# Choosing the first head's experts beside the query projection, and turning the tokens to rows inside the expert stage

## What is computed

```python
qr = (h @ wq).reshape(bsz, t, PEER_HEADS, 2, PEER_HALF)          # 8 heads, 2 x 128 numbers each
scores = einsum('bthpd,hpkd->bthpk', qr, subkeys)                # 128 keys a half
s1, i1 = top_k(scores[..., 0, :], 16);  s2, i2 = top_k(scores[..., 1, :], 16)
cand = s1[..., :, None] + s2[..., None, :]                       # 256 candidates
top, pos = top_k(cand, 16);  eidx = (i1*128 + i2 at pos);  gate = softmax(top)
act = gelu(einsum('ted,td->te', u[eidx], h));  y = einsum('te,ted->td', gate * act, v[eidx])
```

## Time and profile before

| | us |
|---|---|
| median of 3 runs | 4855.84 (4854.93 to 4856.95) |
| the profiled execution, its own time | 4871.88 |
| its span, first to last instruction | 4870.1 |
| PE / DVE / ACT / POOL busy | 3931.9 / 3028.4 / 1902.0 / 1041.7 |
| layer 0: last query column copied to first gather | 693.91 to 716.15 |
| layer 0: gather stream, first issue to last product's start | 716.15 to 2012.90 |
| layer 1: last query column copied to first gather | 2380.08 to 2400.54 |
| layer 1: gather stream, first issue to last product's start | 2400.54 to 3050.28 |

### The profile page before, as it was taken

One profiled execution on the slowest core, in us unless ns is written; L12 is line 12 of the kernel. 1 busy time (PEld: TensorE's weight loads), 2 busy tenths in 40 slices (PEclk: granted clock), 3 DMA queues, 4 the chain that ended last, 5 costly groups with the idle time before them and its releaser, 6 DMA issues. The chain is left out here.

```text
span 4870.1 us, 55663 instructions
## 1 busy us (share of the span) xinstructions
PE 3931.9 (81%) x19683; PEld 2814.8 (58%) x19683; DVE 3028.4 (62%) x6110; ACT 1902.0 (39%) x4173; POOL 1041.7 (21%) x950
## 2 busy tenths in 40 slices
PE   7895677777777777785777777799989998899999
PEld 3574563223232232385532222679988987898899
DVE  7567546676666666467666665546566573565564
ACT  7532313333333333342333333444434353444543
POOL 0006104444344444104144443000010003000000
PEclk9996799999999999997899999979999997899999
DMA  9420139999999999531599999315534550254244
GB/s 374 151 87 0 44 110 421 421 420 417 415 413 418 415 413 418 229 113 32 189 421 421 417 418 415 108 48 165 157 104 135 161 161 5 70 166 148 77 156 139
DMA packets 205623, 1143.57 MB, mean 235 GB/s; under 512 B 23953, under 2 KB 25489, under 8 KB 106529
## 3 DMA queue, kind: packets, MB, share of 16 engines
q0 software_dynamic: 110592, 805.36, 40.0%
q1 hardware_dynamic: 94752, 334.65, 21.0%
HBM read 1138.87 MB, written 1.05 MB: 234 GB/s over the span
## 5 line engine op out<-in xcount | busy, mean ns | idle before, releaser
L1182 PE MATMUL bank<-rows,diag 128*128 128x512 f32 x2304 | 1080.8, 614 | 390.7 <-ACT diag L1237 383.9
L396 PE MATMUL bank<-x_high,w_high 128*128 128x272 f32 (+3 forms) x3560 | 1115.8, 313 | 96.7 <-DVE x_low L479 60.5
L396 PE MATMUL bank<-x_high,w_low 128*128 128x272 f32 (+3 forms) x3560 | 1096.8, 308 | 0.0
L396 PE MATMUL bank<-x_low,w_high 128*128 128x272 f32 (+3 forms) x3560 | 1094.4, 307 | 0.0
L1182 PEld LDWEIGHTS bank<-rows,diag 128*128 128x128 f32 x2304 | 422.7, 193 | 1041.8 <-ACT diag L1237 596.3
L1354 DVE CUSTOM_DVE_ANT_0 junk<-rows,hT 128x1024 f32<-128x1024 f32 x576 | 705.5, 1225 | 408.7 <-DMA rows<-in_peer_uv,expert 398.8
L421 ACT CAST w_high<-ring 128x1024 fp32r<-128x1024 f32 (+2 forms) x541 | 555.9, 1029 | 910.2 <-PE bank L396 897.3
L464 DVE TENSOR_TENSOR w_low<-ring,w_high 128x1024 fp32r<-128x1024 f32 (+2 forms) x541 | 647.8, 1199 | 373.6 <-ACT w_high L421 372.2
L1145 POOL DMA_INDIRECT rows<-in_peer_uv,expert x576 | 612.7, 1064 | 1139.4 <-PE bank L1182 797.2
L396 PEld LDWEIGHTS bank<-x_high,w_high 128*128 128x128 f32 (+1 forms) x3560 | 681.2, 191 | 149.5 <-issue 75.0
L396 PEld LDWEIGHTS bank<-x_low,w_high 128*128 128x128 f32 (+1 forms) x3560 | 682.5, 192 | 23.1
(11 more groups left out here) (394 smaller groups left out, 4601.6 us busy)
## 6 DMA issues: line engine op xcount, KB each, us to landing
ring<-in_w_gate_up SPq DMA_DIRECT2D x176, 512.0 KB, 3.3
ring<-in_w_mod SPq DMA_DIRECT2D x96, 512.0 KB, 5.4
ring<-in_w_in SPq DMA_DIRECT2D x64, 512.0 KB, 3.4
ring<-in_fox_w_in SPq DMA_DIRECT2D x64, 512.0 KB, 3.4
ring<-in_w_down SPq DMA_DIRECT2D x64, 512.0 KB, 3.5
ring<-in_peer_wq SPq DMA_DIRECT2D x32, 512.0 KB, 3.3
ring<-in_gdn_w_in SPq DMA_DIRECT2D x32, 512.0 KB, 3.8
ring<-in_w_down SPq DMA_DIRECT2D x32, 384.0 KB, 3.7
```

The costliest lines, as they stand in the source:

```text
L396: last = pe.matmul(k.bank[c % outs_banks][0:m, 0:nt], w[:, slot, cols], xx[:, t, t0:t0 + nt], start=(t == 0 and n_pass == 0), stop=(t == K ...
L1182: last = pe.matmul(k.bank[2 * (i % 2) + half][:, :], diag[:, n % 4, :], slot(n)[:, D + half * 512:D + (half + 1) * 512], start=(e == 0), s ...
```

## The change

- A class `Choice` holds the keys, the scores and the tiles of the choice; they are allocated before the two streams instead of within the expert stage. Its `choose` is the old one, with `yield 0` for `yield`.
- `stream` gets an SP side. In `peer_wq` SP loads the keys first; PE, after unit 5, forms the scores of head 0's two halves for tile 0; ACT copies them; DVE runs `choose(0)` in pieces.
- The stage `h_rows` is gone. In the expert stage PE turns the tokens to rows after the scores of tile 0, four 128 x 128 blocks to a bank, and ACT copies each bank (128 x 512) to `hT`: eight groups in layer 0, four in layer 1.
- POOL no longer waits for head 0. Gathers 6 and 7, which land in `k.H`, wait until `k.H` is turned (`hrows`). DVE's first product and PE's first sum wait for that too. ACT does head 0's exponentials before the copies of the scores.

```diff
 def stream(k, name, outs, x, evict, signals="", ..., pool_side=None, sp_side=None):
...
         @block.sync
         def _(sp):
+            if sp_side is not None:
+                sp_side(sp, s)
             for u in range(made_from, made_to):
                 sp.wait_ge(k.low_made, count(u))
...
         qr = sbuf(k, es, "qr", [P, 2 * PEER_HEADS, T])
+        choice = Choice(k, es)
...
+            def sp_side(sp, s):
+                sp.dma_start(choice.keys[:, :, :], a.peer_subkeys[l]).then_inc(s.keys, 16)
+
+            def pe_side(pe, s):
+                yield 2
+                pe.wait_ge(s.keys, 16)
+                pe.wait_ge(s.took, 2)
+                for c in range(2):
+                    last = pe.matmul(k.bank[SIDE_BANKS[0]][:, c * P:(c + 1) * P], qr[:, c, 0:P], choice.keys[:, c, :], start=True, stop=True)
+                last.then_inc(s.scored, 1)
+
+            def act_side(act, s):
+                yield 4
+                act.wait_ge(s.scored, 1)
+                act.copy(choice.scores[:, 0:2, :], k.bank[SIDE_BANKS[0]][:, 0:2 * P].rearrange("p (c n) -> p c n", c=2)).then_inc(s.scores, 1)
+
+            def dve_side(dve, s):
+                yield 5
+                dve.wait_ge(s.scores, 1)
+                choice.steps = 0
+                yield from choice.choose(dve, s, 0)
+
             stream(k, "peer_wq", ...,
+                   signals="keys scored scores step spread chosen", pe_side=pe_side, act_side=act_side, dve_side=dve_side, sp_side=sp_side)
-        transpose_chunks(k, "h_rows", [(hT[:, i, c * P:(c + 1) * P], H[:, c, t * P:(t + 1) * P])
-                                       for i, t in enumerate(tiles) for c in range(KD)])
...
-        @block.sync
-        def _(sp):
-            sp.dma_start(keys[:, :, :], a.peer_subkeys[l]).then_inc(s.keys, 16)
...
-                if e % TOPK == 0:
-                    pool.wait_ge(s.chosen, n // TOPK + 1)
+                if e % TOPK == 0 and n > 0:
+                    pool.wait_ge(s.chosen, n // TOPK)
+                if n == SLOTS - 2:
+                    pool.wait_ge(s.hrows, len(groups))
...
-            pe.wait_ge(s.keys, 16)
             score(0)
+            for j, (i, half) in enumerate(groups):
+                if j >= 4:
+                    pe.wait_ge(s.hrows, j - 3)
+                for c in range(4):
+                    last = pe.transpose(k.bank[j % 4][:, c * P:(c + 1) * P], k.H[:, 4 * half + c, tiles[i] * P:(tiles[i] + 1) * P], k.ident)
+                last.then_inc(s.hturned, 1)
...
+            exps(0)
             for n in range(4):
                 take_scores(0, n)
-            exps(0)
+            for j, (i, half) in enumerate(groups):
+                act.wait_ge(s.hturned, j + 1)
+                act.copy(hT[:, i, half * 512:(half + 1) * 512], k.bank[j % 4][:, :]).then_inc(s.hrows, 1)
...
-            for _ in choose(0):
-                pass
             for _ in choose(1):
                 pass
             weigh(0)
...
                 dve.wait_ge(landed[n % SLOTS], 16 * (n // SLOTS + 1))
+                if n == 0:
+                    dve.wait_ge(s.hrows, len(groups))
```

More of the change, by code:

```diff
@@ L1081, in peer, with peer_experts @@
             residual_project(k, "w_out", H, k.mods[:, l, 16:24, :], (1,) if l == DEPTH - 1 else (0, 1))
+            def sp_side(sp, s):
[4 more added lines that the diff above has]
+                pe.wait_ge(s.took, 2)
+                for c in range(2):
+                    last = pe.matmul(k.bank[SIDE_BANKS[0]][:, c * P:(c + 1) * P], qr[:, c, 0:P], choice.keys[:, c, :], start=True, stop=True)
[9 more added lines that the diff above has]
+                yield from choice.choose(dve, s, 0)
             stream(k, "peer_wq", [(1, P, 0, T)] * (2 * PEER_HEADS), H[:, :, T0:T0 + T],
-                   lambda dve, c, bank, s: dve.tensor_copy(qr[:, c, :], bank[:, 0:T]), norm=norm, ahead=False)
+                   lambda dve, c, bank, s: dve.tensor_copy(qr[:, c, :], bank[:, 0:T]), norm=norm, ahead=False,
+                   signals="keys scored scores step spread chosen", pe_side=pe_side, act_side=act_side, dve_side=dve_side, sp_side=sp_side)
         hT = sbuf(k, es, "hT", [P, len(tiles), D])
-        transpose_chunks(k, "h_rows", [(hT[:, i, c * P:(c + 1) * P], H[:, c, t * P:(t + 1) * P])
-                                       for i, t in enumerate(tiles) for c in range(KD)])
-        peer_experts(k, a, l, tiles, qr, hT)
-def peer_experts(k, a, l, tiles, qr, hT):
+        peer_experts(k, a, l, tiles, qr, hT, choice)
+def peer_experts(k, a, l, tiles, qr, hT, choice):
     NH = 2 * PEER_HEADS
@@ L1100, in peer_experts @@
     slots = " ".join(f"landed{n}" for n in range(SLOTS))
-    with ExitStack() as es, stage(k, "experts", slots + " keys scored took step chosen spread grown weights dotted "
+    with ExitStack() as es, stage(k, "experts", slots + " hturned hrows scored took step chosen spread grown weights dotted "
                                   "gelu weighed diag summed out_rows turned added") as (block, s):
         landed = [s.landed0, s.landed1, s.landed2, s.landed3, s.landed4, s.landed5, s.landed6, s.landed7]
-        keys = sbuf(k, es, "subkeys", [P, NH, N_KEYS])
-        scores = sbuf(k, es, "scores", [P, NH, N_KEYS])
         rows = sbuf(k, es, "rows", [P, SLOTS - 2, 2 * D])
@@ L1127, in peer_experts @@
         table = a.peer_uv[l]
+        keys, scores, expert, top, lowest = choice.keys, choice.scores, choice.expert, choice.top, choice.lowest
+        groups = [(i, n) for i in range(NT) for n in range(2)]
         def slot(n):
@@ L1180, in _ @@
                 pe.wait_ge(s.diag, n + 1)
+                if n == 0:
+                    pe.wait_ge(s.hrows, len(groups))
                 for half in range(2):
@@ L1195, in exps @@
             def exps(g):
-                act.wait_ge(s.spread, g + 1)
+                if g > 0:
+                    act.wait_ge(s.spread, g)
                 act.activation(top[:, g % 4, :], top[:, g % 4, :], ACT.Exp, bias=lowest[:, g % 4:g % 4 + 1],
@@ L1319, in weigh @@
+                yield from choice.choose(dve, s, g)
             def weigh(g):
-                nonlocal steps
                 i, h = divmod(g, PEER_HEADS)
```

156 lines of the change are left out of this document (94 added, 62 removed).

## The result

The changed kernel takes **4823.96 us** (median of 4 runs, 4818.93 to 4831.10), the kernel before 4856.4 beside it; the ratio is 0.993 (0.9916 to 0.9940). The forecast was 4815.4, in a range of 4811 to 4826. The gain is 32.4 us instead of 40.4.

A forecast was written before the change was run, and what follows sets the result against it. Gather transfers saturating the DMA engines were taken as the bound. Streams starting 41.30 us earlier, less 0.90 us of PE side work, gave a 40.4 us gain: 4855.84 - 40.4 = 4815.4 us, range 4811 to 4826.

The forecast's parts named there:

- the case called likeliest: Whole kernel: the change works as forecast, gain 38.5 to 42.5 us, time 4813 to 4818; chance 0.70.
- the loop as the pace: Expert stages: the product loop, not the bytes, sets the pace; gain 36.8 us, 4819; chance 0.15 with other small holes.
- side work that shows in layer 1: Layer 1's query projection: DVE's pieces hold up the low halves, costing 9.24 us, 4824.7; chance 0.08 for side work showing.
- What bounds the kernel: Expert stages: gather transfers saturate the DMA engines; only the stream's start and whether it runs dry matter.
- The lead: Last query column to first gather: 22.24 and 20.46 us shrink to 0.70 each, bounds 0.28 and 1.4; 41.30 us saved.
- The streams: Expert stages: each stream lasts as long as before from first issue to last product, 1297 and 650 us.
- Side work: Query projections: PE's added passes cost 0.45 us a layer, 0.9 in all; ACT's copy, DVE's pieces and keys nothing.
- Gather 8: Expert stages: it needs the first pair summed, yet keeps 0.6 to 2.6 us to spare in layer 0; cost zero.
- Gathers 6 and 7: Layer 0's expert stage: they wait for turned rows; gather 6 must issue by 709.8, with 4 to 6 us to spare.
- The rule on the shared port: Early gathers beside choose(1): DVE could block GpSimd's descriptor writes and starve the DMA; one delay uses 0.86 us.

The follow-up runs named there:

- hold: The changed kernel, but GpSimd waits for all turned rows ahead of gather 0 instead of gather 6; 4835.25 us, 0.9945 of the kernel before.
- late: The changed kernel with six extra DVE additions, 4.4 us a layer, ahead of the first product; 4827.14 us, 0.9939 of the kernel before.
- rep: The changed kernel once more, nothing edited; 4826.42 us, 0.9934 of the kernel before.
- rep2: The changed kernel once more, unedited, in the same rounds as best2; 4823.82 us, 0.9940 of the kernel before.
- before_again: The kernel before the change, profiled once more, nothing edited; 4859.48 us, ratio 1.0003.
- a_side: The changed kernel with the separate turning stage put back, the choice kept as side work; 4830.60 us, 0.9934 of the kernel before.
- b_turn: The changed kernel with key load and head 0's choice back in the expert stage, turning kept there; 4855.55 us, 0.9990 of the kernel before.
- best2: best with one early gather in layer 1 instead of three, and tile 0 scored after all turning; 4821.56 us, 0.9933 of the kernel before.
- early: The changed kernel with two gathers per layer issued by GpSimd during the query projection; 4821.59 us, 0.9930 of the kernel before.
- best: early with three early gathers in layer 1, head 1's choice in the row loop, DVE sharing copies; 4824.32 us, 0.9927 of the kernel before.

## Why the prediction was right, and where it was off

The time, 4823.96, lies in the range, but outside the case called likeliest (4813 to 4818). The range reaches above that only to take in two rivals, the loop as the pace (4819) and side work that shows in layer 1 (4824.7), and neither of them happened. So the mechanism is borne out, while it is partly luck that the time still fell in the range: other losses, named below, used up the room that was left for the rivals. A second coincidence: the gain in N-P, 37.1, is nearly the 36.8 of the loop rival. That number alone would speak for the rival; `hold` and `late` decide against it.


- **What bounds the kernel.** Right. `hold` and `late` bracket it: 13.19 us of later first gathers cost 13.20, while 4.4 us of later first product cost 3.1 and 2.5, about what exceeds the 2 us in hand.
- **The lead.** The parts vanished as forecast, but GpSimd starts 1.42 and 1.33 us behind E, not 0.70: the term was mis-sized, and came out at the upper bound given (1.4). It cost 1.35 us. PE starts 0.32 behind E; what GpSimd does in the 1.10 after that, the profile doesn't show.
- **The streams.** "Each stream as long as before": 1298.29 and 650.14 from G to P, against 1296.75 and 649.74: 1.9 us that the sum didn't have. Two profiles of before give 1296.75 and 1297.18 in layer 0, three of the changed kernel 1298.0 to 1298.3, so about 1.2 of it repeat. They don't arise where the change acts. The 193rd product starts 491.45 and 491.93 us behind the first gather in the two profiles of before, and 491.69 to 491.80 in the three of the changed kernel; from there to the last product it is 805.3 against 806.3 to 806.5. A product mostly starts 2.48 us behind the one before, but now and then 2.9 us or more behind it: from the 41st on, that happens 21 times in both profiles of before and 23 times in all three of the changed kernel, at the same products in each. Why it does, and why twice more, stays open.
- **Side work.** PE 0.47 and 0.40 us, forecast 0.45 each. DVE's pieces cost nothing in either layer. In layer 0 DVE stood idle for 6.55 us ahead of a low half, behind ACT, which had waited for PE's side scores; PE never waited for it, since none of its matmuls in the projection starts more than 0.5 us behind the one before:

```profile
641.52 1.23 DVE L466 TENSOR_TENSOR w_low<-ring,w_high 128x1024 fp32r<-128x1024 f32 x1 [6.55 <-ACT w_high L423]
```
```profile
640.17 0.37 ACT L1198 COPY scores<-bank 128x256 f32<-128x256 f32 x1 [10.23 <-PE bank L1192]
```

- **Gather 8.** No dry slot, as forecast, with 2.1 us in hand (0.6 to 2.6). The first product is at E + 11.83, forecast 11.7.
- **Gathers 6 and 7.** No cost, as forecast. They left 11.80 and 13.04 us behind E, and in `rep` 9.29 and 10.56, with E-P the same within 0.04 us; the prediction's limit, 709.8, was 15.9 behind E.
- **The rule on the shared port.** The early gathers, beside `choose(1)`, were issued in 0.94 to 1.16 us each. With DVE busy for nearly all of the time the transfers kept up their rate:

```profile
708.00:712.00 4.00, 0.28 (x1) 0.29 (x2) 3.93 (x17) 1.41 (x6) 0.98 (x2) 0.50 1.01 424
...
716.00:720.00 4.00, 4.00 (x11) 1.75 (x10) 4.00 (x10) 1.65 (x7) 2.44 (x3) 1.00 1.03 424
```

  The gather issued at 718.86, in the second stretch, took GpSimd 1.99 us instead of 0.94, so something delays it. DVE at work isn't enough of a reason, since the gathers at 715.42 and 717.14 took 0.94 each beside a DVE just as busy. The Trainium skill ("SBUF — State Buffer", the box under "SBUF: two separate sides") has GpSimd locked out, and the DMA starve, while DVE holds the port pair that they share. This trace shows a delay and no starving, with several gathers in the queue at the time; which of DVE's instructions here hold the pair, no run shows.
- **What lay outside the sum.** 37.1 us in the expert stretches became 32.4 in the median. About 2.4 are in layer 1's mixer, from layer 0's P to the next N: 306.50 and 306.31 us in the two profiles of before, 308.75, 308.70 and 308.98 in the three of the changed kernel. By the expectation of `rep2` it thus belongs to the kernel and not to one execution. A stretch of it in before and in the changed kernel, placed alike behind P, shows PE at two clocks:

```profile
2192.90:2232.90 40.00, 19.32 (x105) 17.95 (x106) 33.97 (x32) 9.56 (x5) 24.72 (x18) 0.67 0.00 1
```
```profile
2175.02:2215.02 40.00, 20.56 (x96) 19.08 (x96) 31.70 (x29) 8.43 (x5) 22.36 (x16) 0.59 0.00 1
```

  Its code is the same in both, and 0.67 repeats in `before_again`. The edited kernels fall on either side: `a_side` has 306.31, `b_turn` 306.29, `hold` 307.18, `best2` 306.91 and `early` 304.74, but `late` 308.81 and `best` 308.83. So neither the side work nor the turning brings the loss by itself. Here are `a_side` and `rep`, taken in the same rounds, from P to N:

```profile
2006.66:2312.97 306.31, 215.69 (x1225) 187.35 (x1223) 199.30 (x272) 118.76 (x160) 54.23 (x37) 0.84 0.22 72
```
```profile
1992.99:2301.69 308.70, 219.71 (x1225) 191.25 (x1223) 200.18 (x272) 118.67 (x160) 53.84 (x37) 0.82 0.22 71
```

  The granted clock is 0.82 in the five profiles that take 308.7 to 309.0, and 0.83 to 0.85 in the other seven. The forecast carried no term for stages behind the change, and that was its failing assumption. That the lower clock causes the 2.4 us fits the rows, and no run separates it; what lowers the clock stays open. The last 2.3 us (37.1 - 2.4 - 32.4) are of the size by which the medians scatter: the gain is 33.9 in the rounds of `rep` and 33.3 in those of `rep2`.

The miss of 8.6 us is thus 3.3 in the expert stretches (1.35 + 1.9), 2.4 in the mixer, 0.6 because before ran at 4856.4 and not 4855.84 beside it, and 2.3 left over.

## What to carry to other kernels

Where one stream of transfers is saturated, price a change by two numbers: when the first transfer leaves, and by how much the first freed buffer beats the last byte in flight. In this kernel a later start of the product loop cost nothing until the second number, about 2 us, was used up. And a saving of tens of microseconds is seen whole only when the profile is cut at fixed instructions around it, since a later stage, its own code unchanged, can come out longer or shorter at another granted clock: here by 2.4 us from kernel to kernel in one stage, and by 16.6 from one execution of a program to the next in another.

## What the runs showed of the hardware

- A change of stage waits for GpSimd's gathers in flight: stages opened 7.1 us behind the last query column with three in flight (`best`), 4.1 with two (`early`), 1.3 with one that had nearly landed (`best2`), and 0.3 with none or with two that had landed. With gathers in flight they opened 1.4 to 1.8 us behind the end of the transfers. Whether SyncE's transfers do the same, no run here shows.
- The clock granted to TensorE in a stage hangs on more than the stage's own instructions: 323 matmuls took 69.9, 53.3 and 51.3 us at 0.56, 0.80 and 0.84, the first two in the same program.
- A gather's issue on GpSimd mostly takes 0.94 us, and at times 1.7 to 2.0, yet with several gathers in the queue the transfers stayed at a share of about 1.00.
- In a saturated stream of gathers the steps of 2.48 us between products are broken by steps of 3.0 to 3.9 us, at the same products in every execution of a program (21 from the 41st product on in the kernel before, 23 in the changed one).
